# Who issues the DMA that stores the upper weight halves: SyncE or ScalarE

## The reference

```
h = rmsnorm(x) ; z = h @ w_in            # 1024 x 5120, split into u v q f i og gates
a = gmlp(gelu(u), gelu(v))               # 4 heads, 128-position blocks
b = hgrn2(q, f, i, og)                   # 4 heads, 128 x 128 state, chunks
y = sigmoid(ga) * (a @ w_br_gm) + sigmoid(gb) * (b @ w_br_hg)
x = x + y @ w_out
h = rmsnorm(x) ; z = conv3(h @ w_up)     # 1024 x 5632
x = x + (silu(gate) * val) @ w_down      # 2816 x 1024
out = rmsnorm(x)
```

## Time and profile before

| | us |
|---|---|
| median of 3 runs | 2908.93 (2903.7 to 2910.54) |
| profiled execution, its time | 2908.73 |
| its span | 2906.9 |
| TensorE busy | 2877.3 (99%) |
| VectorE busy | 1479.7 (51%) |
| ScalarE busy | 715.8 (25%) |
| GpSimd busy | 195.9 (7%) |
| first tile (split of weights) | 0 to about 740 of the span |
| DMA queue q1, all transfers | 612.46 MB, 59.6% of 16 engines' span |

### The profile page before, as it was taken

The page is one execution under the profiler, slowest core; times in us unless marked ns, Lnnn a source line. Parts: engine busy times, 40 slices in busy tenths (PEclk is TensorE's granted clock), DMA queues, the critical chain, the costliest instruction groups (busy, mean ns, idle before and its releaser), DMA issues.

```text
span 2906.9 us, 33466 instructions
## 1 busy us (share of the span) xinstructions
PE 2877.3 (99%) x13344; PEld 2393.6 (82%) x13344; DVE 1479.7 (51%) x2878; ACT 715.8 (25%) x980; POOL 195.9 (7%) x87
## 2 busy tenths in 40 slices
PE   8999999999999999999999999999999999999998
PEld 6888888888888888888888888888888888888886
DVE  6876677755266434553326634455323663355521
ACT  5332244433122112221112211222111211122210
POOL 3323410014000000000000000000000000000000
PEclk9999999999999999999999999999999999999999
DMA  8656988889743465556563445555656345555554
GB/s 297 232 175 234 321 282 290 291 305 318 256 156 144 160 219 189 198 191 231 203 221 141 151 175 212 187 200 190 231 206 215 137 142 198 203 190 199 190 206 170
DMA packets 121978, 614.59 MB, mean 211 GB/s; under 512 B 13536, under 2 KB 13792, under 8 KB 74080
## 3 DMA queue, kind: packets, MB, share of 16 engines
q1 hardware_dynamic: 121824, 612.46, 59.6%
HBM read 474.00 MB, written 138.41 MB: 211 GB/s over the span
## 4 chain that ended last, share of the span: by engine, by line
PE 94%; DVE 2%; issue 2%; DMA 1%; POOL 1%; ACT 0%; SPq 0%; POOLq 0%; DVEq 0%; ACTq 0%
PE bank L968 27%; PE bank L969 27%; PE bank L973 27%; PE bank L1029 3%; PE bank L1016 2%; PE bank L1018 2%; PE bank L1017 1%; DMA raw<-w_units 1%; PE bank L1105 1%; POOL w_both L402 1%; PE bank L982 1%; PE bank L979 1%; PE bank L980 0%; DMA w_split<-w_both 0%; PE bank L1134 0%
## 5 line engine op out<-in xcount | busy, mean ns | idle before, releaser
L968 PE MATMUL bank<-h_hi,w_both 128*128 128x512 f32 x2400 | 947.4, 395 | 0.0
L969 PE MATMUL bank<-h_lo,w_both 128*128 128x512 f32 x2400 | 935.2, 390 | 0.0
L973 PE MATMUL bank<-h_hi,w_both 128*128 128x512 f32 x2400 | 593.5, 389 | 0.0
L968 PEld LDWEIGHTS bank<-h_hi,w_both 128*128 128x128 f32 x2400 | 451.4, 188 | 97.2 <-issue 4.8
L969 PEld LDWEIGHTS bank<-h_lo,w_both 128*128 128x128 f32 x2400 | 451.2, 188 | 97.0 <-issue 4.8
L973 PEld LDWEIGHTS bank<-h_hi,w_both 128*128 128x128 f32 x2400 | 450.6, 188 | 93.7
L890 DVE TENSOR_TENSOR z<-bank,rms_inv 128x512 f32<-128x512 f32 x176 | 121.8, 692 | 354.1 <-PE bank L973 346.4
L968 PE MATMUL bank<-g_hi,w_both 128*128 128x512 f32 x704 | 275.4, 391 | 0.0
L969 PE MATMUL bank<-g_lo,w_both 128*128 128x512 f32 x704 | 273.9, 389 | 0.0
L903 DVE SCALAR_TENSOR_TENSOR conv<-z,params,conv 128x512 f32<-128x512 f32 x352 | 263.6, 750 | 7.0 <-DVE halo L893 0.8
L402 POOL TENSOR_TENSOR w_both<-raw,w_both 128x1024 fp32r<-128x1024 f32 x80 | 194.8, 2435 | 540.3 <-ACT w_both L416 499.0
(11 more groups left out here) (203 smaller groups left out, 3130.2 us busy)
## 6 DMA issues: line engine op xcount, KB each, us to landing
w_both<-w_split SPq DMA_DIRECT2D x372, 1024.0 KB, 4.8
w_split<-w_both SPq DMA_DIRECT2D x248, 512.0 KB, 5.7
raw<-w_units SPq DMA_DIRECT2D x124, 512.0 KB, 5.4
x_in<-x_t SPq DMA_DIRECT2D x32, 256.0 KB, 5.6
res<-x_t SPq DMA_DIRECT2D x32, 256.0 KB, 5.1
out<-res SPq DMA_DIRECT2D x32, 256.0 KB, 6.9
masks<-masks_in SPq DMA_DIRECT2D x1, 1152.0 KB, 9.7
gm_w<-gm_wt SPq DMA_DIRECT2D x1, 256.0 KB, 6.5
```

The lines of the kernel that those rows point to most:

```text
L968: pe.matmul(dst, w_hi[slot][:, off + k, :], rhs_hi(k), start=first and k == 0, stop=False)
L969: pe.matmul(dst, w_hi[slot][:, off + k, :], rhs_lo(k), start=False, stop=False)
L973: mm = pe.matmul(dst, w_lo[slot][:, off + k, :], rhs_hi(k), start=False, stop=last and k == n - 1)
```

## The change

In the first tile the wait for hi_made and the store of the upper half leave SyncE's `first_tile` and stand in ScalarE's program directly behind the cast that makes the half. Sizes, addresses and semaphores of the store stay.

```diff
         def first_tile(u):
             s = u % 2
-            sp.wait_ge(hi_made, u + 1)
-            sp.dma_start(w_split[u, :, 0, :, :].bitcast(F32), w_hi[s].bitcast(F32)).then_inc(hi_out[s], 16)
             sp.wait_ge(lo_made, u + 1)
             if u + 2 < UNITS:
                 load_raw(u + 2)
@@
             act.wait_ge(hi_out[slot], 16 * (u // 2 + 1))
             act.activation(w_hi[slot], raw[slot][:, :, :], ACT.Copy).then_inc(hi_made, 1)
+            send_upper(u + 2)
+
+        def send_upper(u):
+            act.wait_ge(hi_made, u + 1)
+            act.dma_start(w_split[u, :, 0, :, :].bitcast(F32), w_hi[u % 2].bitcast(F32)).then_inc(hi_out[u % 2], 16)
@@
         def first_weights(j):
             act.wait_ge(raw_in[j], 16)
             act.activation(w_hi[j], raw[j][:, :, :], ACT.Copy).then_inc(hi_made, 1)
+            send_upper(j)
```

## The result

The changed kernel takes 2914.62 us (median of 19 runs, 2910.61 to 2923.83), the kernel before 2906.26 us (19 runs, 2902.46 to 2911.04). The ratio is 1.0029, 95% interval 1.0022 to 1.0037: 8.4 us slower, with 2912.3 forecast from a profiled execution of 2908.73. The time lies in the stated range, but the step was forecast as 3.6 us and is 8.4, so more than half of it has to be found.

A forecast was written before the change was run, and what follows sets the result against it. TensorE was taken as the bound, busy 2877.3 of 2906.9 us. Terms 1.6 + 0.45 + 0.4 + 1.15 = 3.6 us gave span 2910.5, plus 1.8 is 2912.3; own range 2910.5 to 2916, full range 2906 to 2921.

The forecast's parts named there:

- What is removed: SyncE in the first tile loses 124 waits and 124 issues of 0.32 us; nothing ends there, worth 0.
- One issue on ScalarE: After each of 124 casts, an issue of 0.320 us delays a following table load by 0.40, a sigmoid by 0.48.
- Heads' ends: Behind each head's last cast, table load, gelu and square delay TensorE's next matmul: four times 0.40, 1.6 us.
- start of head 0: ScalarE's unbroken run of two casts ends 0.80 later against 0.35 of room before TensorE: 0.45 us, once.
- first up unit: Cast, table load, square root and VectorE's diagonal, for which TensorE already waits, come later: 0.40 us, once.
- Early 1.15 us: Chain from unit 2's raw load to the first token sum: 0.9 + 0.48 - 0.24 later.
- the 0.4 taken off: Early stage: unit 0's store runs beside pure loads, which moved 361 GB/s against 422 mixed; raw 2 0.4 us sooner.
- The last term, 0.48 - 0.24: Early chain: ScalarE's send behind the cast costs 0.48 more, less 0.24 of room before GpSimd's start.
- The other reading in the prediction: Early stage: issuing from several engines saves only issuing time, so raw 2 does not move; early term 0.24.
- Down stage worth 0: Later tile 0 loads have room: a raw landing 1.25 later still leaves 1.5 before TensorE wants the cast.
- Rival 1: Loads starve in the down stage once raws land after more than 6.4 us: 15 us lost, 2927; chance 0.08.
- rival 2: Clock: new idle at heads' ends, or any shift, brings one more half-clock drop, 5.2 us, 2917.5; chance 0.13.

The follow-up runs named there:

- e11_repaired: Kernel before, but ScalarE issues upper stores of units 2 to 99, in heads and at first up unit behind work TensorE waits for; 2904.15 us, ratio 0.9995.
- e7_sends_late: Kernel before, but ScalarE issues upper stores of units 9 to 33, placed behind the sigmoids, squares or gelus instead of the casts; 2906.10 us, ratio 0.9999.
- e2_heads: Kernel before, but ScalarE issues only the upper stores of units 9 to 33, whose casts stand in the heads; 2907.20 us, ratio 0.9999.
- e4_middle: Kernel before, but ScalarE issues the upper stores of units 2 to 99, SyncE the rest; 2907.47 us, ratio 0.9999.
- e1_early: Kernel before, but ScalarE issues only the upper stores of units 0 and 1; 2907.71 us, ratio 0.9999.
- e5_store_first: Kernel before, one queue, but SyncE issues the upper store of unit 1 ahead of the raw load of unit 2; 2907.59 us, ratio 1.0006.
- e3_down: Kernel before, but ScalarE issues only the upper stores of units 100 to 123, the down projection; 2910.72 us, ratio 1.0012.
- e8_x_spread: As e3_down, but tile 0 issues the eight x loads one with each of 8 units instead of two with each of 4; 2910.85 us, ratio 1.0013.
- e6_raw_first: Kernel before, one queue, with each raw load ahead of the upper store of the unit before it; 2917.73 us, ratio 1.0040.
- e9_masks_late: Kernel before, with the 1152 KB masks load moved from ahead of unit 2's raw load to behind unit 1's lower store; 2903.57 us, ratio 0.9989.
- e12_x_short: As e3_down, but tile 1's x loads bring 128 of 512 tokens, VectorE filling the rest with ones; 2906.61 us, ratio 0.9999.
- e10_early_masks_late: As e9_masks_late, and ScalarE issues the upper stores of units 0 and 1; 2904.56 us, ratio 0.9995.

## Why the prediction was right, and where it was short

- *What is removed is worth 0.* Held. e11_repaired and e7_sends_late take stores from SyncE at no cost and gain nothing.
- *One issue on ScalarE: 0.32 us, delay 0.40 and 0.48.* Measured 0.326, table load 0.39 after the cast. The forecast that the sigmoids' delay doesn't reach TensorE held: the four flips wait 4.6 us in all, 5.0 before.
- *Heads' ends 1.6, start of head 0 0.45, first up unit 0.40.* Measured for the first two together +1.6 (e2_heads, 2.05 expected); waits of 0.2 and 0.4 for the single places. e4_middle, which holds all three, has +2.2 against 2.45.
- *Early 1.15 us.* Right in mechanism and mis-sized: 1.7 corrected, 2.0 in the trace. Raw 2 landed 2.0 later (13.1 and 13.3 us against 11.2 from nearly the same issue), above the upper end of 1.25. The one store ahead of it was counted rightly, at 1.25. Wrong is the 0.4 taken off because stores would run beside pure loads: the engines, as full as before, moved less and not more, 315 GB/s over the first 21 us in the changed kernel and 322 in e1_early, against 333 before and 328 to 335 in the seven other kernels with the same early order on one queue. As an estimate from these rates, 18 and 11 GB/s over 21 us are 0.38 and 0.23 MB, at 422 GB/s 0.9 and 0.5 us; with one store that is about the measured 2.0 and 1.8. Why they moved less no run shows; e5_store_first, on one queue, has 319. The last term, 0.48 - 0.24, didn't show: from raw 2's landing to the token sum it takes 10.1 us in both kernels. The other reading in the prediction, raw 2 not moved and an early term of 0.24, falls.
- *Down stage worth 0.* This step failed: "A raw that lands 1.25 later leaves 1.5." It read one cast and its room before TensorE. The load issued at 663.5 took 8.4 us, and the chain that broke is another one: the raws hold ScalarE, whose squares of x are queued behind the cast and feed the second token sum, for which TensorE had already waited 0.22 us before. Measured +2.5, and 1.3 of clock with it. Rival 1 (loads starve) named the place and that the engines are full there, but priced it at 15 us and gave it 0.08; its point, landings above 6.4 us, was passed by single loads, not by all (median 5.3).
- *Clock.* The forecast had no term; rival 2 had one drop more, 5.2 us. On the mean of the 19 runs it took some 2 us more than from before. The runs show where a part of it comes from: the down stage's wait. Behind a token sum that waited 2.4 or 2.5 us the profiled executions lose 1.7 us to half clock (changed kernel, e3_down), behind 3.4 us they lose 3.4 (e8_x_spread), behind 0.2 nothing; and over their runs e3_down and e8_x_spread lost 1.3 and 2.0 more than before, e1_early, e2_heads and e4_middle 0.8 to 2.1 less. Whether the change makes a second head drop more often, as in the execution shown, is open.
- The sum: early 1.7, the rest of the first stages 2.2, down 2.5, clock about 2, together 8.4. The medians differ by 8.4 and the means by 8.3.
- *Own range 2910.5 to 2916* holds 2914.62. It was helped by luck with its base: the profiled execution of before was 2.5 us above the median of 19, and on that median the same own range would have been 2908.0 to 2913.5, too low.

## What to carry to other kernels

A wait that is read with room to spare has to be followed past the instruction that waits: what is queued behind it on its engine has its own consumer and its own room, and here there was none: TensorE already waited 0.2 us for it. Issuing part of the transfers from another engine added no bandwidth here, where the DMA engines were full; it changed who goes first, and the loads in the old queue paid 1.3 to 2 us each where TensorE hung on them. Put an issue behind the work that others wait for, not behind the instruction whose result it sends; and before transfers are spread over queues, take out of the queue's head what isn't needed yet (1152 KB of masks were worth 2.5 us).

## What the runs showed of the hardware that I had not expected

- A DMA issue on ScalarE that had nothing to wait for cost its program nothing: 0.33 us beside running activations (153.37 in e7_sends_late), and the table load behind it began 0.02 us after the square. With a wait for its own cast in front, the same issue held the next instruction up by 0.39 us.
- A store issued later on a second queue landed before a load issued earlier on the first: 18.7 against 22.9 us, issued at 11.15 and 9.60.
- Flip waits of the same 1.2 us lead to half clock after head 2 (before), after heads 2 and 3 (changed kernel), after head 0 (e6_raw_first, e9_masks_late, e12_x_short), after head 3 (e10_early_masks_late) or after none (the other eight), at some 5 us each. Over 33 runs of before the times have a standard deviation of 2.2 us, and 1.1 once the clock is taken out.
